# Per-head attention epilogue, causal masks, z units and first merge groups rearranged in a fused attention and convolution layer

## What is computed

```python
h = rms_norm(x, norm_pre_w)
q, k, v, z_a, u_glu, z_c, ga, gc = jnp.split(h @ w_in, split_points, axis=-1)
# branch A: two softmax maps per head, 8 heads, value width 128
a = softmax(mask(q0 @ k0.T)) - lam * softmax(mask(q1 @ k1.T))      # causal mask
o = a @ v
o = rms_norm(o, subln_w) * (1 - lam_init)                          # per head
y_attn = (o * silu(z_a)) @ w_o_attn
# branch B: GLU, causal depthwise conv of 31, LayerNorm
u = silu(layer_norm(conv(u_glu))) * silu(z_c)
y_conv = u @ w_pw2 + b_pw2
m = sigmoid(ga) * y_attn + sigmoid(gc) * y_conv
x = x + rms_norm(m @ w_out)
```

## Time and profile before

| | |
|---|---|
| time, median of 3 runs | 1184.86 us (1184.51 to 1188.22) |
| the profiled execution | 1188.11 us |
| its spans | core 0: 1186.5, the seven others 1177.3 to 1179.4 us |
| busy on core 0 | PE 1100.3 us (93%), DVE 548.2 (46%), ACT 323.9 (27%), POOL 102.0 (9%) |
| attention, core 0 | from 417.5 to 668 us |
| attention, core 1 | from 448.6 to 777.5 us |
| merge and output, core 0 | from 668 us to the end |
| merge and output, core 1 | from 777.5 us to the end |

### The profile page before, as it was taken

How to read it: one execution, slowest core, us unless ns; L and a number is a source line. 1 busy time by engine, 2 the same in 40 slices (tenths; PEclk the granted TensorE clock), 3 DMA queues, 4 the chain that set the end, 5 groups by cost and what they waited for, 6 DMA issues and landing times.

```text
span 1186.5 us, 21787 instructions; the slowest of 8 cores (1177.3 to 1186.5 us)
## 1 busy us (share of the span) xinstructions
PE 1100.3 (93%) x8042; PEld 675.6 (57%) x8042; DVE 548.2 (46%) x1287; ACT 323.9 (27%) x500; POOL 102.0 (9%) x196
## 2 busy tenths in 40 slices
PE   2699999999999998899878899999999999999995
PEld 1356556886666774577444466666666666654442
DVE  5564444426644236766777533333333333315333
ACT  3442223432011165466444311111111111102111
POOL 1111010010201100000000001101101010000000
PEclk9799999999999998899899899999999999999998
DMA  8928758553755622322142315236275283164442
GB/s 250 222 41 163 154 104 158 104 87 73 133 111 109 138 57 57 56 43 52 40 72 37 48 24 108 42 66 105 46 135 98 45 143 49 23 178 160 155 162 94
DMA packets 49359, 116.93 MB, mean 99 GB/s; under 512 B 5472, under 2 KB 11872, under 8 KB 45920
## 3 DMA queue, kind: packets, MB, share of 16 engines
q0 software_dynamic: 27648, 62.93, 32.6%
q1 hardware_dynamic: 21312, 52.35, 14.2%
q10 hardware_dynamic: 288, 0.18, 0.0%
HBM read 161.76 MB, written 16.58 MB: 150 GB/s over the span
## 4 chain that ended last, share of the span: by engine, by line
PE 82%; DVE 8%; issue 3%; ACT 3%; DMA 1%; DVEq 0%; SPq 0%; ACTq 0%
PE ps L1276 21%; PE ps L649 11%; PE ps L816 11%; PE ps L1328 10%; PE ps L770 10%; PE ps L1286 5%; PE ps L1280 5%; PE ps L693 3%; PE ps L922 2%; PE ps L1021 2%; PE ps L899 2%; DVE r L958 1%; DVE r L1028 1%; DVE zoz L970 1%; DMA r<-usc 1%
## 5 line engine op out<-in xcount | busy, mean ns | idle before, releaser
L1276 PE MATMUL ps<-hTo,wring 128*128 128x384 bf16 x1536 | 257.7, 326 | 0.0
L1276 PEld LDWEIGHTS ps<-hTo,wring 128*128 128x128 bf16 x1536 | 150.4, 98 | 99.5 <-issue 0.5
L164 POOL DMA_DIRECT2D wring<-wp x176 | 93.3, 548 | 842.3 <-PE ps L1276 243.4
L649 PE MATMUL ps<-hTo,wring 128*128 128x384 bf16 x768 | 135.2, 339 | 10.1 <-ACT hTo L545 4.2
L770 PE MATMUL ps<-wring,hTo 128*128 128x256 bf16 x1152 | 136.3, 273 | 1.3 <-PE ps L899 1.2
L1293 ACT ACTIVATE zoz<-zoz 128x384 f32<-128x384 f32 x96 | 50.1, 523 | 316.7 <-DVE zoz L1291 316.7
L816 PE MATMUL ps<-hTo,wring 128*128 128x384 bf16 x768 | 125.0, 326 | 0.0
L770 PEld LDWEIGHTS ps<-wring,hTo 128*128 128x128 bf16 x1152 | 108.8, 98 | 21.6 <-issue 8.5
L649 PEld LDWEIGHTS ps<-hTo,wring 128*128 128x128 bf16 x768 | 77.0, 102 | 66.3 <-issue 21.2
L1291 DVE TENSOR_TENSOR zoz<-ps,R 128x384 f32<-128x384 f32 x96 | 53.5, 558 | 128.6 <-PE ps L1276 128.6
L905 ACT ACTIVATE r<-ps 128x1024 bf16<-128x1024 f32 (+2 forms) x104 | 92.8, 905 | 47.2 <-PE ps L899 43.7
(11 more groups left out here) (114 smaller groups left out, 1014.6 us busy)
## 6 DMA issues: line engine op xcount, KB each, us to landing
...
```

What stands on the lines that cost most here:

```text
L164: eng.dma_start(out=it[1][0], in_=it[1][1]).then_inc(self.dsem[it[2]], 16)
L649: t.op('pe', lambda e, dc=dc, x=x: e.matmul(bank(2 * par + x, n), lhsT=w[:, dc, 128 * x:128 * x + 128], rhs=hTo[:, dc, c:c + n], start=(dc ...
L1276: t.op('pe', lambda e, dc=dc, k=k, w=w, o=o, cs=cs, c0=c0, n=n: e.matmul(o[k], lhsT=w[:, dc, cs], rhs=hTo[:, dc, HALO + c0:HALO + c0 + n], ...
```

## The change

Five edits. All stand within attention and the first two groups of the merge.

1. `finalize` now copies each slot into one buffer of the head (`acc`), and the normalization runs over a part of the head at once: tiles 0 to 5 and 6 to 8 on even cores, 0 to 2 and 3 to 6 on odd ones (`H.part`). All steps are plain two-operand operations over the whole part; the sum of squares is a product and a reduction, the last scaling two products for each part. `H.rate` becomes 3 and 2.
2. On even cores the mask is added by a matmul (identity times a block with -30000 above the diagonal) into the scores before the exponential; the DVE multiplication goes. Odd cores keep it.
3. The z units are in all quarters: chunks 0-1, 2-3, 4, 5-7 on even cores (6, 6, 3 and 9 units), 0, 1, 2-3, 4-7 on odd ones (2, 2, 4 and 8). Two weight panels change places for it.
4. The two DVE operations that follow a z unit's tanh go to a list `zlate` and are issued after the scores of the next step.
5. Gates and convolution branch of merge groups 0 and 1 are issued before the transposes of heads 6 and 7, which use two banks instead of four.

```diff
-    p += [rng(C_V), rng(C_V + 256), rng(C_ZC), rng(C_V + 512), rng(C_V + 768), rng(C_ZC + 256), rng(C_ZC + 512), rng(C_ZC + 768)]
+    p += [rng(C_V), rng(C_V + 256), rng(C_ZC), rng(C_V + 512), rng(C_ZC + 256), rng(C_V + 768), rng(C_ZC + 512), rng(C_ZC + 768)]
...
-            self.rate = 6
+            self.rate, self.part = 3, {2: (0, 6), 4: (6, 9)}
+            self.fill = ((('v', 1), ('z', 0, 1)), (('v', 2), ('z', 2, 3)), (('v', 3), ('z', 4)), (('z', 5, 6, 7),))
...
-            self.rate = 4
+            self.rate, self.part = 2, {1: (0, 3), 3: (3, 7)}
+            self.fill = ((('v', 1), ('z', 0)), (('z', 1), ('v', 2)), (('z', 2, 3), ('v', 3)), (('z', 4, 5, 6, 7),))
...
-    osb = [m.f32(128 * NT).rearrange("p (i n) -> p i n", i=NT) for k in range(2)]
-    accs = [m.f32(520)[:, 0:516].rearrange("p (b c n) -> p b c n", b=2, c=2) for k in range(4)]
-    t0s = m.f32(256).rearrange("p (b n) -> p b n", b=2)
+    acc = [m.f32(NT * 258).rearrange("p (i c n) -> p i c n", i=NT, c=2) for k in range(2)]
...
+            add = masked and half == 0
             for c in range(2):
-                t.op('pe', lambda e, kt=kt, qo=qo, qn=qn, o=o, c=c: e.matmul(
+                t.op('pe', lambda e, kt=kt, qo=qo, qn=qn, o=o, c=c, add=add: e.matmul(
                     bank(pb + c, qn, o), lhsT=KT[hp][64 * c:64 * c + 64, 128 * kt:128 * kt + 128],
-                    rhs=QT[hp][64 * c:64 * c + 64, 128 * q0 + qo:128 * q0 + qo + qn], start=True, stop=True),
-                    reads=rd, writes=[('ps', pb + c)], sig=(k == len(ent) - 1 and c == 1))
+                    rhs=QT[hp][64 * c:64 * c + 64, 128 * q0 + qo:128 * q0 + qo + qn], start=True, stop=not add),
+                    reads=rd, writes=[('ps', pb + c)], sig=(not add and k == len(ent) - 1 and c == 1))
+            if add:
+                for c in range(2):
+                    t.op('pe', lambda e, o=o, c=c: e.matmul(bank(pb + c, 128, o), lhsT=ident, rhs=neg, start=False, stop=True),
+                         reads=['cb'], writes=[('ps', pb + c)], sig=(k == len(ent) - 1 and c == 1))
...
-            if masked:
+            if masked and half == 1:
...
+    zlate = []
+    def run_zlate():
+        while zlate:
+            zlate.pop(0)()
...
-        while late and late[0][0] <= fk - 4:
+        while late and late[0][0] <= h - 2:
             run_late(1)
-        ac, an = accs[fk % 4][:, 0:nq], ('accs', fk % 4)
-        rs = rsv[:, fk, 0:nq, :]
-        ob = osb[h % 2]
+        ac = acc[h % 2]
+        an = [('acc', h % 2, i) for i in range(q0, q0 + nq)]
+        dst = ac[:, q0:q0 + nq]
         src = ps[:, 2048:2048 + 512 * nq].rearrange("p (b c n) -> p b c n", b=nq, c=2)[:, :, :, 0:129]
         if half == 0:
-            t.op('act', lambda e: e.activation(out=ac, in_=src, func=AF.Copy), reads=[('ps', 4 + b) for b in range(nq)], writes=[an])
+            t.op('act', lambda e: e.activation(out=dst, in_=src, func=AF.Copy), reads=[('ps', 4 + b) for b in range(nq)], writes=an)
         else:
-            t.op('dve', lambda e: e.tensor_copy(out=ac, in_=src), reads=[('ps', 4 + b) for b in range(nq)], writes=[an])
-        f = [lambda: t.op('dve', lambda e: e.reciprocal(out=rs, in_=ac[:, :, :, 128]), reads=[an, 'small'], writes=[('rs', fk)]),
+            t.op('dve', lambda e: e.tensor_copy(out=dst, in_=src), reads=[('ps', 4 + b) for b in range(nq)], writes=an)
+        if si not in H.part:
+            return
+        i0, i1 = H.part[si]
+        n = i1 - i0
+        names = [('acc', h % 2, i) for i in range(i0, i1)]
+        a0, a1 = ac[:, i0:i1, 0, 0:128], ac[:, i0:i1, 1, 0:128]
+        rs = rsv[:, h % 2, i0:i1, :]
+        rn = ('rs', h % 2, i0)
+        def tt(out, x, y, op, rd, wr):
+            return lambda: t.op('dve', lambda e: e.tensor_tensor(out=out, in0=x, in1=y, op=op), reads=rd, writes=wr)
+        f = [lambda: t.op('dve', lambda e: e.reciprocal(out=rs, in_=ac[:, i0:i1, :, 128]), reads=names + ['small'], writes=[rn]),
              lambda: t.op('dve', lambda e: e.tensor_scalar(out=rs[:, :, 1], in0=rs[:, :, 1], scalar1=neglam, scalar2=None, op0=ALU.mult),
...
+                          reads=[rn, 'neglam'], writes=[rn]),
+             tt(a0, a0, rs[:, :, 0:1].to_broadcast([128, n, 128]), ALU.mult, names + [rn], names),
+             tt(a1, a1, rs[:, :, 1:2].to_broadcast([128, n, 128]), ALU.mult, names + [rn], names),
+             tt(a0, a0, a1, ALU.add, names, names),
+             tt(a1, a0, a0, ALU.mult, names, names),
+             lambda: t.op('dve', lambda e: e.tensor_reduce(out=ssqh[:, h, i0:i1], in_=a1, axis=AX.X, op=ALU.add),
+                          reads=names + ['small'], writes=[('ssqh', h, i0)])]
         if si == NS - 1:
...
+            f += rsqrt_ops(rstdh[:, h, 0:NT], ssqh[:, h, 0:NT], NT, 1.0 / 128, 1e-5, [('ssqh', h, x[0]) for x in H.part.values()], [('rstdh', h)])
+            for j0, j1 in H.part.values():
+                nm = [('acc', h % 2, i) for i in range(j0, j1)]
+                oz = [('oz', i, h) for i in range(j0, j1)]
+                v = zoz[:, j0:j1, 128 * h:128 * h + 128]
+                b0 = ac[:, j0:j1, 0, 0:128]
+                f += [tt(b0, b0, rstdh[:, h, j0:j1].unsqueeze(2).to_broadcast([128, j1 - j0, 128]), ALU.mult, nm + [('rstdh', h)], nm),
+                      tt(v, b0, v, ALU.mult, nm + oz, oz)]
+            f.append(lambda: oz_done.add(h))
+        late.extend((h, x) for x in f)
...
+            run_zlate()
             run_late(H.rate)
...
+                run_zlate()
                 t.op('dve', lambda e: e.tensor_tensor(out=zv, in0=bank(b, n), in1=rv, op=ALU.mult), reads=[('ps', b)] + rn, writes=[('zt', p)])
                 t.op('act', lambda e: e.activation(out=sv, in_=zv, func=AF.Tanh, scale=0.5), reads=[('zt', p)], writes=['zs'])
-                t.op('dve', lambda e: e.scalar_tensor_tensor(out=zv, in0=sv, scalar=1.0, in1=zv, op0=ALU.add, op1=ALU.mult),
-                     reads=[('zt', p), 'zs'], writes=[('zt', p)])
-                t.op('dve', lambda e: e.tensor_tensor(out=uv, in0=uv, in1=zv, op=ALU.mult),
-                     reads=[('zt', p), ('u2T', cc, g)], writes=[('u2T', cc, g)])
+                zlate.append(lambda: t.op('dve', lambda e: e.scalar_tensor_tensor(out=zv, in0=sv, scalar=1.0, in1=zv, op0=ALU.add, op1=ALU.mult),
+                                          reads=[('zt', p), 'zs'], writes=[('zt', p)]))
+                zlate.append(lambda: t.op('dve', lambda e: e.tensor_tensor(out=uv, in0=uv, in1=zv, op=ALU.mult),
+                                          reads=[('zt', p), ('u2T', cc, g)], writes=[('u2T', cc, g)]))
...
+        if g == 3:
             t.handover(oth_res + lnbuf + ['cw', ('lj', 0), ('lj', 1)], ozT_all + [('wop', 0)] + ([('wop', 1)] if NX else []))
...
+        turns = [f for h in range(6) for f in oz_turns(h, fb)]
+        for what in H.fill[g]:
+            if what[0] == 'v':
+                for u in units(0, NK):
+                    fill += v_unit(what[1], u, fb)
+            else:
+                zcu = [(cc, k) for cc in what[1:] for k in range(NG)]
+                for n, (cc, k) in enumerate(zcu):
+                    fill += zc_pieces(cc, k, fb)
+                    if g == 3 and n >= 2:
+                        for _ in range(-(-len(turns) // (len(zcu) - n))):
+                            fill.append(turns.pop(0))
+        assert g < 3 or not turns
...
+    run_zlate()
...
-        tb = Banks([6, 7, 4, 5])
+        tb = Banks([2, 6])
...
+        for k, w, slot in ((0, wga, sa), (1, wgc, sc)):
+            for dc in range(16):
+                t.op('pe', lambda e, dc=dc, k=k, w=w: e.matmul(
+                    bank(b0 + k, n), lhsT=w[:, dc, cs], rhs=hTo[:, dc, HALO + c0:HALO + c0 + n], start=(dc == 0), stop=(dc == 15)),
+                    reads=[('W', slot, dc // 4)] + own_res, writes=[('ps', b0 + k)], sig=(dc == 15))
+        for fc in range(8):
+            t.op('pe', lambda e, fc=fc: e.matmul(
+                bank(b0 + 3, n), lhsT=wopb[pi % 2][:, 1, fc, cs], rhs=uT[:, fc, 32 + c0:32 + c0 + n], start=(fc == 0), stop=(fc == 7)),
+                reads=[('wop', pi % 2)] + [('u2T', c, tg) for c in range(8)], writes=[('ps', b0 + 3)], sig=(fc == 7))
...
+    def merge_tail(it, pi, ci, tg):
...
+                bank(b0 + 2, n), lhsT=wopb[pi % 2][:, 0, fc, cs], rhs=ozT[:, fc, c0:c0 + n], start=(fc == 0), stop=(fc == 7)),
+                reads=[('wop', pi % 2)] + ozT_all, writes=[('ps', b0 + 2)], sig=(fc == 7))
...
+                if it == 0:
+                    merge_head(0, 0, 0, 0)
+                    merge_head(1, 0, 0, 1)
+                    f_begin()
+                elif it > 1:
+                    merge_head(it, pi, ci, tg)
+                merge_tail(it, pi, ci, tg)
```

118 lines of the change are left out of this document (32 added, 86 removed).

## The result

The changed kernel takes 1188.8 us (median of 19 runs) against 1186.1 us before (19 runs). The ratio is 1.0022, with a 95% interval of 1.0013 to 1.0032: slower by 0.2%, within the 0.3% that the prediction counts as no difference. The forecast of 1172 us and its range, 1165 to 1181, were wrong.

The account below looks back on a forecast made before the run. Late DVE operations stalling PE in attention bound both programs. Even cores gain 19 us (core 0 at 1167), odd 8.5 (core 1 last at 1170.5); plus 1.6 gives 1172 us, range 1165 to 1181.

Parts of the forecast that it names:

- What bounds the kernel: In attention both core programs matter; late DVE operations stall PE: 27.3 us on core 0, 8.3 on core 1.
- Part 1: Normalization by parts on even cores: DVE busy sum unchanged, fewer starts take 10 us off DVE, between -2 and 18.7.
- rival (d): Bursts of normalization operations stall both programs, core 1 losing 7 us instead of gaining 8.5: 1188 us, chance 0.05.
- Part 2: Mask matmuls on even cores: 20.9 us off DVE, 8.6 us more work for PE, between 0 and 12.
- Part 3: Z units by quarter: even quarter 4 gives up 6 of 15, odd 2 of 10; odd waits 2 us less.
- Rival (a): Odd cores keep stalls: transposes two behind every z unit, parts ahead of copies; 1178 to 1181 us, chance 0.17.
- Part 4: Held-back pair: odd cores save 6 us of slot-copy waits, between 2 and 8.3; even cores nothing.
- Part 5: Merge order around the transposes: 1 us saved on either program, between -1 and 1.7.
- The clock: Slow clock in attention returns as stalls go: 9 of up to 15.7 us on even cores, 2 on odd.
- What would show it: Signs if right: even attention 225 to 235 us, no stall over 3 us, odd quarter 4 about 78 us.
- rival (b): Odd cores get quarter 4 as full as quarter 3, 14 us gained, even cores at 1164: 1166 us, chance 0.12.

Follow-up runs that it names:

- no_norm: The changed kernel with the slot-by-slot normalization of before put back, all else as changed: 1187.9 us.
- Norm: Edit 1, normalization by parts of a head; as the one edit on the kernel before: 1193.1 us.
- fill: Edit 3, z units in all quarters with the order of panels; the changed kernel without it: 1184.3 us.
- three_rate: The kernel before with mask matmuls, held-back z pair and merge order, at rates 5 and 3 for 6 and 4: 1184.9 us.
- the skip: No deferred operation issued in the step that ends a slot; as the one edit on the kernel before: 1190.5 us.
- the skip pair: The changed kernel with the skip and rate 4 on even cores, 1179.7 us, against norm_skip, 1173.7 us.
- only_mask: The kernel before with one edit, the masks of even cores by matmuls: 1185.4 us.
- three: The kernel before with three edits, mask matmuls, held-back z pair and merge order: 1181.1 us.
- z: Edit 4, the held-back pair behind a z unit's tanh; as the one edit on the kernel before: 1187.3 us.
- only_norm: The kernel before with one edit, the normalization by parts of a head: 1193.1 us.
- norm_skip: three_skip with normalization by parts of a head added, rate 4 and 2: 1173.7 us.
- three_skip: As three, with no deferred operations in a slot's last step: 1173.8 us.

## Why the prediction was wrong

**What bounds the kernel: right.** Both programs mattered, and most of the stalls were late operations on DVE.

**Part 1: the step that failed.** The price of one operation was right (0.954 us forecast, 0.958 measured over six tiles; 0.558 and 0.557 over three):

```profile
L970 DVE TENSOR_TENSOR r<-r,small 128x768 f32<-128x768 f32 x24 | 23.0, 958 | 2.3
L970 DVE TENSOR_TENSOR r<-r,small 128x384 f32<-128x384 f32 x24 | 13.4, 557 | 1.7
```

DVE was relieved too, by 8.0 us of busy time on core 2 (145.65 us in no_norm to 137.66): I had left the small operations out of the sum (L949 and L950 took 15.5 us on core 2 before; L971 and L972 take 6.5). But I turned work taken off DVE into time by proportion: 31 us less work was to end 18 of 27.3 us of stalls on even cores and give back 9 us of slow clock. DVE did become 25.6 us lighter on core 2, and core 0 lost 9.9 us of its waits, while its PE was busy 11.1 us longer in attention (226.88 us for 215.78), where the sum has the mask matmuls and the faster clock all but cancel out. Norm itself gave no time: nothing on even cores, and 8.2 us lost on odd ones. What counts is which operation stands ahead of the slot copy or a z unit when it is due. A slot's operations were issued in the two steps behind it and the queue was mostly empty at the next slot's end; a part's queue is up to 25 operations long at two a step, and lies across two slot ends of each head. I had the mechanism as rival (d), "the same bursts stall both programs", 1188 us, with a chance of 0.05, and argued it away with quarter 3's full PE at the old rate, which says nothing on a backlog at the new one. That its 1188 us came out is in part luck: it has norm's bursts alone at work, and fill, by another path, cost 4.6 us of the odd cores' loss. What should have been counted is which operations are issued in a slot's last step, and whether any are left by then; three_rate shows that the reach of the queue alone does not tell.

**Part 2: right in kind, mis-sized.** 11.1 us for 8.6, still within my 0 to 12. If they cost as much in every kernel, then the lighter DVE gave back 18.2 us for that in the changed kernel (7.1 net) and 13.3 alone (2.2 net).

**Part 3: wrong.** I gave odd cores a third of the waits not named, and took fuller quarters as free. Even cores pay 4.2 us in the changed kernel and 7.8 without norm (631.2 to 623.4), but 0.9 with the skip; odd ones 4.6, 3.7 and 10.8. On odd cores quarter 3 takes the two units at their full price (6.2 us, 78.4 to 84.6 in the skip pair), and in quarter 4 the pairs of transposes eat what leaves it (83.4 us for 79.7). Rival (a) named these pairs ("two behind every z unit"), and I let the order of DVE speak against it, which shows the copy ahead of the held-back pair, not ahead of the bursts.

**Part 4: right on odd cores alone** (5.7 us measured, 6 forecast). In the changed kernel part operations took the pair's place ahead of the copy, and the wait stayed at 10.1 us. On even cores alone it cost 4.8 us, not nothing; core 2 waits 12.4 us for the exponential there, up to 4.9 at a time (10.8 and 4.2 before), and why has not been followed.

**Part 5: near nothing**, inside its range of -1 to 1.7 us. From only_mask to three the merge goes from 378.5 to 378.7 us on even and from 293.3 to 293.4 on odd cores; z came in with it, which alone made the merge 1.0 and 0.9 us longer, so the two are not parted. The waits around the transposes on core 2 went from 1.7 us before to 1.9, now for copies out of the two banks. It seems to hide the rest that norm leaves: only_norm's merge is 382.5 and 298.1 us long, the changed kernel's 378.7 and 293.4.

**The clock.** It came back only in part on even cores (0.94 to 0.96 over attention on core 0). Three stalls of 3.0 to 4.0 us remained, and behind them, from 481.15 to 486, 547 to 552 and 602.6 to 608 us, the granted clock was 0.50, 0.66 and 0.73; between them it was 1.00. With the long stalls gone from attention it is higher: the mean clocks of even cores over their whole span are 0.986 to 0.990 in norm_skip, for 0.974 to 0.982 before.

**What would show it.** "No stall over 3 us" was wrong (4.03), and waits of odd PE for L1021 above 5 us were named as the sign of a wrong prediction: 5.1. Attention on even cores took 250.6 us on core 2, not 225 to 235; quarter 4 of odd cores 85.2 us, not 78, at a clock of 0.96 on core 3; the copy L959 was waited for 7.5 us, not under 3; an even core ended last. Waits for L1044 under 5 us (2.6) and a lighter DVE were right, and did not bring the time. One number of the prediction has no sum behind it: rival (b) has the even cores at 1164 where its own sum has them at 1167.

A time near the forecast of 1172 us was to be had, but with the skip, which the forecast did not contain: three_skip and norm_skip take 1173.8 and 1173.7 us, both 1.1% below the kernel before, with even cores last in most runs.

What stays open: why z alone costs even cores 4.8 us, why the skip is worth so much more to them in the changed kernel (16.0 us) than beside three edits (6.1), and which work would shorten them below 617 us. The costs of the edits do not add (norm on odd cores: +11.2, +8.2 or -3.5 us, by what stands beside it), so no single number is the price of an edit.
